# Strassen-like down products: seven block products for eight in four feed-forward groups

## The reference

```
h = rmsnorm(x, norm_ffn[i])
gu = h @ ffn_w_in[i]                       # 1024 -> 2 x 2816
x = x + (silu(gu[:, :2816]) * gu[:, 2816:]) @ ffn_w_out[i]
```

## Time and profile before

| | |
|---|---|
| median of 3 runs | 2080.69 us (2080.11 to 2082.2) |
| span of the profiled execution | 2080.3 us |
| PE busy | 2041.6 us, 98% |
| DVE busy | 965.7 us, 46% |
| ACT busy | 780.6 us, 38% |
| POOL busy | 324.6 us, 16% |
| mean granted TensorE clock | 0.997 |

### The profile page before, as it was taken

How to read it: one execution, slowest core, us unless ns; L and a number is a source line. 1 busy time by engine, 2 the same in 40 slices (tenths; PEclk the granted TensorE clock), 3 DMA queues, 4 the chain that set the end, 5 groups by cost and what they waited for, 6 DMA issues and landing times.

```text
span 2080.3 us, 26716 instructions
## 1 busy us (share of the span) xinstructions
PE 2041.6 (98%) x10149; PEld 1656.0 (80%) x10149; DVE 965.7 (46%) x1969; ACT 780.6 (38%) x1552; POOL 324.6 (16%) x497
## 2 busy tenths in 40 slices
PE   7999999999999999999999999999998999999998
PEld 6887888888888886788888888888787888777766
DVE  5437434443354345435534443364435664535455
ACT  4226332222232222333322222243337884435453
POOL 1103100000011120000110000041003764312211
PEclk9999999999999999999999999999999999999999
DMA  5330243333324331133243333225321103423212
GB/s 179 104 99 11 63 133 95 99 91 101 93 81 142 91 101 41 53 99 97 69 132 99 97 96 99 93 83 160 119 75 58 32 22 102 114 74 109 66 47 81
DMA packets 96910, 187.32 MB, mean 90 GB/s; under 512 B 8423, under 2 KB 16655, under 8 KB 96656
## 3 DMA queue, kind: packets, MB, share of 16 engines
q1 hardware_dynamic: 90432, 164.35, 26.3%
q0 software_dynamic: 6352, 21.27, 3.2%
HBM read 181.33 MB, written 4.26 MB: 89 GB/s over the span
## 4 chain that ended last, share of the span: by engine, by line
PE 90%; ACT 5%; DVE 2%; issue 1%; POOL 1%; DMA 0%; SPq 0%; ACTq 0%; DVEq 0%; POOLq 0%
PE bank L754 62%; PE bank L790 9%; PE bank L1265 5%; PE bank L1024 2%; PE bank L1186 1%; PE bank L1163 1%; PE bank L828 1%; PE bank L1279 1%; ACT sc L1808 1%; PE bank L1009 1%; PE bank L1095 1%; PE bank L1302 1%; PE bank L853 1%; ACT xn L1802 1%; PE bank L1152 1%
## 5 line engine op out<-in xcount | busy, mean ns | idle before, releaser
L1979 DVE TENSOR_TENSOR wl<-raw,wh 128x1024 fp32r<-128x1024 f32 x306 | 376.7, 1235 | 771.9 <-ACT wh L1382 770.9
L1382 ACT ACTIVATE wh<-raw 128x1024 fp32r<-128x1024 f32 x306 | 320.9, 1053 | 827.3 <-PE bank L754 785.5
L754 PE MATMUL bank<-hTh,wh 128*128 128x512 f32 (+2 forms) x1200 | 467.5, 390 | 0.2 <-issue 0.2
L754 PE MATMUL bank<-hTl,wh 128*128 128x512 f32 (+2 forms) x1200 | 466.9, 389 | 0.0
L754 PE MATMUL bank<-hTh,wl 128*128 128x512 f32 (+2 forms) x1200 | 466.9, 389 | 0.0
L754 PEld LDWEIGHTS bank<-hTh,wh 128*128 128x128 f32 (+2 forms) x1200 | 223.9, 187 | 48.7 <-issue 0.3
L754 PEld LDWEIGHTS bank<-hTh,wl 128*128 128x128 f32 (+2 forms) x1200 | 223.9, 187 | 48.2
L754 PEld LDWEIGHTS bank<-hTl,wh 128*128 128x128 f32 (+2 forms) x1200 | 223.9, 187 | 47.9
L754 PE MATMUL bank<-wh,hTh 128*128 128x512 f32 x400 | 156.5, 391 | 0.1
L754 PE MATMUL bank<-wh,hTl 128*128 128x512 f32 x400 | 155.7, 389 | 0.0
L754 PE MATMUL bank<-wl,hTh 128*128 128x512 f32 x400 | 155.6, 389 | 0.0
(11 more groups left out here) (383 smaller groups left out, 3105.5 us busy)
## 6 DMA issues: line engine op xcount, KB each, us to landing
raw<-in_ffn_w_in SPq DMA_DIRECT2D x88, 512.0 KB, 3.7
raw<-in_ret_w_in SPq DMA_DIRECT2D x48, 512.0 KB, 3.8
raw<-in_ffn_w_out SPq DMA_DIRECT2D x44, 512.0 KB, 3.7
raw<-in_diff_w_in SPq DMA_DIRECT2D x32, 512.0 KB, 3.7
raw<-in_fox_w_in SPq DMA_DIRECT2D x24, 512.0 KB, 4.1
raw<-in_nsa_w_in SPq DMA_DIRECT2D x20, 512.0 KB, 3.7
raw<-in_ret_w_out SPq DMA_DIRECT2D x16, 512.0 KB, 3.7
raw<-in_fox_w_out SPq DMA_DIRECT2D x8, 512.0 KB, 3.7
```

The source lines that it names most:

```text
L754: i = pe.do.matmul(dst, x, y, start=first and k == 0 and q == 0, stop=stop)
L1382: act.do.activation(M.hl[n % HL_SLOTS][0][:, 0:m], M.raw[n % RAW_SLOTS][:, 0:m], ACT.Copy).then_inc(*T.up("act_hi", n))
L1979: dve.do.tensor_tensor(wl[:, 0:m], M.raw[n % RAW_SLOTS][:, 0:m], wh[:, 0:m].bitcast(F32), ALU.subtract).then_inc(*T.up("dve_lo", n))
```

## The change

For groups 1 to 4 of each layer the product A (512 tokens x 512 hidden) by B (512 x 1024) is cut into 2 x 2 blocks each way, A in blocks of 256 x 256 and B in blocks of 256 x 512, and the four blocks of the result are made of seven block products, in Winograd's form:

- DVE makes sums of weight blocks: T1 = B12 - B11, T2 = B22 - T1, T3 = B22 - B12, T4 = B21 - T2, in place in the raw buffers, T2 in a buffer `form`. Four loads make seven chunks to split, in the order B11, T2, T1, B21, T3, B22, T4. A raw buffer is held until the last chunk that it carries is split.
- DVE makes sums of blocks of `f.pr`, S1 to S4, in place; ACT and DVE split each as before. For the first two tiles of a take only the first 256 tokens need `ah` and `al` then.
- PE works seven steps of 12 matmuls (2 token tiles x 2 x 3) into three pairs of banks: X for steps 0 and 3, Y for 1, 4 and 6, W for 2 and 5. A bank goes on being summed into from step to step, and DVE reads it after each step: step 0 goes to a buffer `alpha`, the others to `X`. `alpha` is summed over the four groups and added to `X` by six additions ahead of down(5).
- In DVE's program the four sums follow up(g)'s last split, the low halves of S1 and S3 stand ahead of step 0's evictions of down(g - 1), those of S2 and S4 ahead of step 1's, and a split follows each step's two evictions.

The core of the diff:

```diff
+SEVENS = (1, 2, 3, 4)
+STEPS = (("X", "A11"), ("Y", "S2"), ("W", "S1"), ("X", "A12"), ("Y", "S3"), ("W", "S4"), ("Y", "A22"))
+INTO = ("alpha", (0, 1), (2, 1), (0, 0), (2, 1), (0, 1), (2, 0))
+SUMS = {"T1": ("B11", "B12", "B11", "B11"), "T2": ("form", "B22", "B11", "T1"), "T3": ("B12", "B22", "B12", "B12"),
+        "T4": ("B21", "B21", "form", "T2")}
+QUADS = ("B11", "B12", "B22", "B21")
+SEVEN = ("B11", "T2", "T1", "B21", "T3", "B22", "T4")
+HELD = {"B11": "T1", "B12": "T3", "B22": "B22", "B21": "T4"}
+AFTER = {"B11": ("T1", "T2", "T3"), "B21": ("T4",)}
...
+    def seven(name, r0, rows, halves):
+        first, n = len(loads), len(chunks)
+        where = {q: first + k for k, q in enumerate(QUADS)}
+        last = {q: n + SEVEN.index(HELD[q]) for q in QUADS}
+        for q in QUADS:
+            loads.append((name, r0 + rows * (int(q[1]) - 1), rows // 128, (halves[int(q[2]) - 1],), last[q]))
+        for form in SEVEN:
+            chunks.append((rows // 128, halves[0][1], where, form, n))
...
@@ ffn(): down(g) of weight_chunks
+            if g in SEVENS:
+                seven(f"ffo{i}", c0, 256, ((0, 512), (512, 512)))
+                return
...
@@ ffn buffers
+        f.s = {form: [(sb(stack, "sh", [128, 2, 256], F32R), sb(stack, "sl", [128, 2, 256], F32R)) for _ in range(2)]
+               for form in ("S1", "S2", "S4")}
+        f.alpha, f.form = sb(stack, "alpha", [128, 2, S]), sb(stack, "form", [128, 1024])
...
@@ load_weights(n)
-            sp.wait_ge(*at("act_hi", n - RAW_SLOTS))
-            sp.wait_ge(*at("dve_lo", n - RAW_SLOTS))
+            last = LOADS[n - RAW_SLOTS][4]
+            sp.wait_ge(*at("act_hi", last))
+            sp.wait_ge(*at("dve_lo", last))
+            if CHUNKS[last][3] is not None:
+                sp.wait_ge(*at("dve_form", (CHUNKS[last][4], "T3")))
...
+def pe_seven(pe, T, M, tag, operand, ready):
+    first4, next4 = pe.banks4(), pe.banks4()
+    banks = T.bank[tag] = {"X": first4[0:2], "Y": first4[2:4], "W": next4[0:2]}
+    seen = {}
+    for j, (where, form) in enumerate(STEPS):
+        n = pe.use
+        pe.use += 1
+        wh, wl, nk = chunk_views(M, n)
+        h, l = operand(form)
+        for r in range(2):
+            b, cols = banks[where][r], slice(r * 128, r * 128 + 128)
+            if where in seen:
+                pe.wait_ge(*T.at("dve_seven", (tag, seen[where], r)))
+            else:
+                pe_bank(pe, T, b)
+            pe_weights(pe, T, n)
+            for name, key in ready(form):
+                pe.wait_ge(*T.at(name, key))
+            for k in range(nk):
+                for q, (x, y) in enumerate([(h[:, k, cols], wh[:, k, :]), (h[:, k, cols], wl[:, k, :]), (l[:, k, cols], wh[:, k, :])]):
+                    end = k == nk - 1 and q == 2
+                    i = pe.do.matmul(M.bank[b][:, :], x, y, start=where not in seen and k == 0 and q == 0, stop=end, skip_group_check=True)
+            i.then_inc(*T.up("pe_product", (tag, j, r), *[("chunk", n)] * r))
+            pe.free[b] = [("dve_seven", (tag, j, r))]
+        seen[where] = j
...
+def seven_form(f, g, form):
+    a, b = f.ah[g % 2], f.al[g % 2]
+    if form in f.s:
+        return [x[:, :, :] for x in f.s[form][g % 2]]
+    ks, ts = {"A11": (0, 0), "A12": (2, 0), "S3": (0, 256), "A22": (2, 256)}[form]
+    return a[:, ks:ks + 2, ts:ts + 256], b[:, ks:ks + 2, ts:ts + 256]
...
@@ act_ffn, take_up and the stage of g
-            act.do.activation(f.ah[g % 2][:, o, :], f.pr[:, o, :], ACT.Copy).then_inc(*up("act_ah", (i, g, o)))
+                act.wait_ge(*at("pe_product", down_end(i, g - 2)))
+            n = S // 2 if g in SEVENS and o < 2 else S
+            act.do.activation(f.ah[g % 2][:, o, 0:n], f.pr[:, o, 0:n], ACT.Copy).then_inc(*up("act_ah", (i, g, o)))
+    def high(g, form):
+        act.wait_ge(*at("dve_sum", (i, g, form)))
+        act.do.activation(seven_form(f, g, form)[0], seven_sum(f, form), ACT.Copy).then_inc(*up("act_s", (i, g, form)))
-        for half in range(2):
-            act_product(act, T, M, FFG[g - 1][1] // 256)
+        splits = 7 if g - 1 in SEVENS else FFG[g - 1][1] // 128
+        for c in range(splits):
+            if g in SEVENS and c < 2:
+                for form in (("S1", "S3"), ("S2", "S4"))[c]:
+                    high(g, form)
+            act_split(act, T, M)
...
@@ dve_split
+    for form in AFTER.get(CHUNKS[n][3], ()):
+        dve_sum(dve, T, M, n, form)
+def dve_sum(dve, T, M, n, form):
+    nk, width, where, own, first = CHUNKS[n]
+    x, y = SUMS[form][1:3]
+    for q in (x, y):
+        if q in where:
+            dve.wait_ge(*T.at(f"raw{where[q] % RAW_SLOTS}", where[q]))
+    dve.wait_ge(*T.at("dve_lo", n))
+    if form != "T1":
+        dve.wait_ge(*T.at("dve_form", (first, {"T2": "T1", "T3": "T2", "T4": "T2"}[form])))
+    if form == "T2" and dve.formed is not None:
+        dve.wait_ge(*T.at("dve_lo", dve.formed + SEVEN.index("T2")))
+        dve.wait_ge(*T.at("dve_form", (dve.formed, "T4")))
+    out, a, b = (form_buffer(M, where, q)[:, 0:nk * width] for q in (SUMS[form][0], x, y))
+    dve.do.tensor_tensor(out, a, b, ALU.subtract).then_inc(*T.up("dve_form", (first, form)))
+    if form == "T4":
+        dve.formed = first
...
@@ dve_ffn
+            if g - 1 in SEVENS:
+                dve.wait_ge(*at("dve_s", (i, g - 1, "S4")))
-            dve.do.tensor_tensor(f.al[g % 2][:, o, :], f.pr[:, o, :], f.ah[g % 2][:, o, :].bitcast(F32), ALU.subtract).then_inc(
+            n = S // 2 if g in SEVENS and o < 2 else S
+            dve.do.tensor_tensor(f.al[g % 2][:, o, 0:n], f.pr[:, o, 0:n], f.ah[g % 2][:, o, 0:n].bitcast(F32), ALU.subtract).then_inc(
                 *up("dve_al", (i, g, o)))
+    def sums(g):
+        q11, q12, q21, q22 = (f.pr[:, k:k + 2, t:t + 256] for t in (0, 256) for k in (0, 2))
+        dve.wait_ge(*at("dve_al", (i, g, 3)))
+        dve.do.tensor_tensor(q22, q21, q22, ALU.add).then_inc(*up("dve_sum", (i, g, "S1")))
+        dve.wait_ge(*at("dve_sum", (i, g, "S1")))
+        dve.do.tensor_tensor(q21, q11, q21, ALU.subtract).then_inc(*up("dve_sum", (i, g, "S3")))
+        dve.wait_ge(*at("dve_sum", (i, g, "S3")))
+        dve.do.tensor_tensor(q11, q22, q11, ALU.subtract).then_inc(*up("dve_sum", (i, g, "S2")))
+        dve.wait_ge(*at("dve_sum", (i, g, "S2")))
+        dve.do.tensor_tensor(q12, q12, q11, ALU.subtract).then_inc(*up("dve_sum", (i, g, "S4")))
+
+    def low(g, form):
+        h, l = seven_form(f, g, form)
+        dve.wait_ge(*at("act_s", (i, g, form)))
+        dve.do.tensor_tensor(l, seven_sum(f, form), h.bitcast(F32), ALU.subtract).then_inc(*up("dve_s", (i, g, form)))
+
+    def evict(g, j, r):
+        tag = f"down{i}{g}"
+        where = STEPS[j][0]
+        src = M.bank[T.bank[tag][where][r]][:, :]
+        dve.wait_ge(*at("pe_product", (tag, j, r)))
+        if INTO[j] == "alpha":
+            if g == SEVENS[0]:
+                dve.do.tensor_copy(f.alpha[:, r, :], src).then_inc(*up("dve_seven", (tag, j, r)))
+            else:
+                dve.wait_ge(*at("dve_seven", (f"down{i}{g - 1}", j, r)))
+                dve.do.tensor_tensor(f.alpha[:, r, :], f.alpha[:, r, :], src, ALU.add).then_inc(*up("dve_seven", (tag, j, r)))
+            return
+        t, half = INTO[j][0] + r, INTO[j][1]
+        xs = M.X[:, t, half * 512:half * 512 + 512]
+        dve_x_newest(dve, T, t)
+        dve.do.tensor_tensor(xs, xs, src, ALU.add).then_inc(*up("dve_seven", (tag, j, r)))
+        dve.x[t] = ("seven", (tag, j, r))
+
+    def merge(t):
+        r, tag = t % 2, f"down{i}{SEVENS[-1]}"
+        dve.wait_ge(*at("dve_seven", (tag, 0, r)))
+        for half in ((1,), (0, 1))[t // 2]:
+            xs = M.X[:, t, half * 512:half * 512 + 512]
+            dve_x_newest(dve, T, t)
+            dve.do.tensor_tensor(xs, xs, f.alpha[:, r, :], ALU.add).then_inc(*up("dve_x", (f"merge{i}", t, half)))
+            dve.x[t] = (f"merge{i}", t, half)
 
...
@@ dve_ffn, the loop over g
     for g in range(1, 6):
         dve_product(dve, T, M, 4)
         dve_product(dve, T, M, 4, 4, take_up(g))
+        if g in SEVENS:
+            sums(g)
+        if g - 1 in SEVENS:
+            for j in range(7):
+                if g in SEVENS and j < 2:
+                    for form in (("S1", "S3"), ("S2", "S4"))[j]:
+                        low(g, form)
+                for r in range(2):
+                    evict(g - 1, j, r)
+                dve_split(dve, T, M)
+            continue
         for half in range(2):
             dve_product(dve, T, M, FFG[g - 1][1] // 256, 4, dve_add(dve, T, M, f"down{i}{g - 1} {half}", half))
+            if g in SEVENS:
+                for form in (("S1", "S3"), ("S2", "S4"))[half]:
+                    low(g, form)
+    for t in range(4):
+        merge(t)
     if i == 0:
         a, b = (dve_add_and_scale(dve, T, M, "n2", f"down05 {half}", half) for half in range(2))
```

More of the change, by code:

```diff
@@ L70, with plain @@
 FFG = [(0, 256)] + [(256 + g * 512, 512) for g in range(5)]
-def weight_chunks():
-    chunks = []
```

(53 more changed lines are left out.)

22 lines of the change are left out of this document (14 added, 8 removed).

## The result

| | before | after |
|---|---|---|
| median, four runs each | 2081.28 us | 2101.59 us |
| ratio to before, 95% interval | | 1.0093 [1.0081, 1.0105] |
| span of the profiled execution | 2080.3 | 2101.6 |
| PE busy | 2041.6 | 2035.0 |
| DVE busy | 965.7 | 1097.2 |

A forecast was written before the change was run, and what follows sets the result against it. PE bounds the feed-forward, but in changed down stages DVE's queue of evictions holds it. Terms 17.4 - 2.5 + 1.9 = +16.8 us on 2080.3 gave 2097.1, stated as 2097.5; range 2084 to 2107, with rivals 2080 to 2110.

The forecast's parts named there:

- DVE's queue: Full down stage: takes, sums, low halves, evictions and splits timed from the up product's end; step 4's eviction at 21.05 us.
- Waits ahead of steps 3, 4 and 6, none ahead of 5: Full down stage: PE waits for DVE's evictions to free banks, about 3 us ahead of step 3, again before 4 and 6.
- +2.98 a full stage, +2.5 the first: Changed down stages that also hold sums and low halves: PE leaves 2.98 us later, in layer 0's first 2.5.
- -1.23 a fourth stage: Each layer's last changed stage, in group 5, without sums or low halves: PE leaves 1.23 us sooner, -2.5 for two.
- T1 to T3 at nothing: Gate product's last slot: three weight sums, 3.7 us, fit where DVE idles 4.2 us, so they cost nothing.
- Layer 0's tail +1.9: Last down of layer 0: alpha merges delay the first tile's additions and norm, stalling PE's transpose by 1.9 us.
- Layer 1's tail: nothing: Last down of layer 1: the merges' delay costs nothing, as a wait for PE's second tile lies before the norm.
- The price of chaining: DVE's queue: a 128x512 op waiting for the one before costs 0.72 to 0.73 us against 0.60; without it 2094.5 us.
- Rival (c): Clock falls after PE's wait before step 3: +1 to +3 us in six stages, 2104 to 2116 us; chance 0.11.
- If the granted clock falls: Full down stage: one of the listed signs that the forecast is wrong, TensorE's granted clock falling.
- (a): Full stages: evictions come in time, PE never waits, -22.0 + 1.9, so 2060.6 us, faster; chance 0.13.
- (b): Full stages: DVE's queue 2.5 to 3 us shorter through cheaper sums and takes, about the same, 2081 us; chance 0.08.

The follow-up runs named there:

- t4_early: Changed kernel with activation sums behind the seven steps, alpha merges split around tile 0's additions, and T4 formed one slot sooner on DVE: 2060.71 us, 0.9895 of before.
- own_bank: Changed kernel with a pair of banks of its own for step 6, no longer waiting for step 4's eviction: 2096.06 us, 1.0071 of before.
- late_sums: Changed kernel with only the four activation sums and their eight halves moved behind the seven steps: 2069.61 us, 0.9941 of before.
- no_t123: Changed kernel without T1, T2 and T3, T4 staying as B21 - B12: 2100.58 us, 1.0091 of before.
- no_t4: Changed kernel without T4, B21 split and used in its place: 2090.38 us, 1.0044 of before.
- spread: Changed kernel with the six alpha merges moved from ahead of the last down's additions to just ahead of each token tile's: 2103.19 us, 1.0104 of before.
- pool_t4: Changed kernel with activation sums behind the seven steps, alpha merges split around tile 0's additions, and T4 on POOL: 2067.62 us, 0.9932 of before.
- only_four: Changed kernel with seven products in group 4 alone, groups 1 to 3 by eight products: 2086.03 us, 1.0019 of before.

## Why the prediction was right, and where its sizes were off

- **A matmul saved is 0.229 us, 2.75 a stage.** Right: t4_early shows exactly that once nothing waits, 62.75 for 65.50.
- **DVE's queue.** Right, op by op: the takes began at -1.88 (said: -1.94), the sums at 6.61 (6.54), step 0's eviction at 10.60 (10.53), step 4's at 21.13 (21.05). The sums cost like low halves, 0.68 to 0.69, chained 0.73.
- **Waits ahead of steps 3, 4 and 6, none ahead of 5.** Right where the clock stays up: 3.19, 0.51, 1.22 us. In the four stages where it fell PE waits ahead of steps 3 and 6 alone, and leaves at the same time. own_bank shows that step 6 waits for the bank of step 4, late_sums that the order of DVE's queue sets how long.
- **+2.98 a full stage, +2.5 the first, -1.23 a fourth stage.** Measured 3.00 to 3.02, 2.39, -1.22 and -0.94; in layer 1's fourth stage PE waited 0.44 us ahead of step 3, which I had not in the sum.
- **T1 to T3 at nothing.** Right (no_t123), and T4 at its full length (no_t4: 1.3 us a group, said 1.27).
- **Layer 0's tail +1.9.** It was +2.15; the stall itself was 1.88.
- **Layer 1's tail: nothing.** Wrong, +1.87 us; the step that failed is "a wait for PE's second tile lies between, so nothing". I compared the first tile's norm with DVE's additions and left out who stands between them. The root there is a chain of ten small ops on POOL, two norms deep. Its first op for tile 0 began at 1399.17, which is 9.7 us after the start of the last down (7.4 before the change), and DVE's scaling waited for its last one until 1404.96; PE waited 0.31 us. From then on POOL is the one that is late. PE's four transposes began 16.5, 25.6, 31.9 and 38.3 us after the start of the last down before the change, and 17.0, 26.3, 33.3 and 40.1 after. With the merges spread over the tiles (spread) the chain began at 7.4 again and 1.27 of the 1.87 us were back. The chain of waits in the changed kernel runs over POOL in this stretch:

```profile
1411.81 2.46 POOL cells L516
...
1414.34 0.58 POOL cells L518
...
1415.02 2.16 POOL cells L520
```

In the kernel before the ops of L516 and L520 (L460 and L464 there) took 0.30 and 0.34 us in the median. But in this very stretch its ops were long too, up to 2.28 us: all forty took 22.4 us there and 24.8 after. That DVE's crowded queue makes POOL's small ops long is suggested by pool_t4, not shown here.

- **The terms and the rest.** 2.39 + 3.02 + 3.01 + 3.01 + 3.00 + 3.02 = 17.45 (said 17.4); -2.16 (-2.5); 2.15 (1.9); 1.87 (0). That is 19.3 of the 21.3 us. The other 2.0 are the two stretches without changed work; of the 4.5 us by which the spans differ more than my sum of 16.8, they and layer 1's tail make 3.9. In the sparse attention's start the clock was at 0.50 from 1600 to 1610, as it had been 0.67 after the long wait before; how long it stays low there differs between executions, and what of the 1.26 us it makes up is not settled.
- **The price of chaining.** The trace sides with the earlier trace rows: 452.20 to 452.92 is 0.72 for an op of 0.68 that the next waits for, against 0.60 from 454.99 to 455.59, between two ops of the same size in SBUF that do not wait. The Trainium skill (VectorE: DVE Perf Modes, section The DRAIN you can't avoid) has it that a semaphore behind each op costs nothing extra. The trace does not agree where the next op waits for it: 0.12 us each here.
- **Rival (c), and a sign of being wrong that came.** "If the granted clock falls" stands among the signs of being wrong, and it fell in four of the six full stages: in four of the five in which PE had idled 3.2 us, and not in the first, after 2.59. So half of rival (c) came true, and the forecast's time held because the price in these stages was nought, for the reason that own_bank shows. I had reckoned with six slow microseconds and an extra of 1 us or more; a spell was some eight matmuls long, and the waits ahead of steps 4 and 6 took in what it cost. The Trainium skill (TensorE: Matmul & The Clock Gate, section HAM oscillation) puts a limit to the idle gaps of PE, and the waits here stay under it. So the prediction's step from that page to "(c) would hold in every full stage" was not sound. Nor does the trace agree with the limit: the clock fell behind four of these shorter waits.
- **Rivals (a) and (b)** fell with the queue as worked out. The time of (a), 2060.6, is what t4_early reached with 2060.71, once the evictions do start in time; that the two agree to a tenth is luck, since its tails differ from (a)'s terms.

## What to carry to other kernels

Fewer products on the busiest engine are worth what the queue that must empty their banks allows: list that queue op by op from the last moment at which it was idle, and look at when it reaches the eviction that PE waits for, not at the engine's share. Before giving up such a change, move everything in that queue that nobody waits for yet behind the evictions, and into idle slots; here the same work in another order turned +1% into -1%. A stretch that hangs on a chain of small ops on a third engine has no slack but that engine's own.

## What the runs showed of the hardware that I had not expected

- TensorE's granted clock fell to 1.2 GHz behind some stalls of PE and not behind others of the same length. After 3.2 us it fell in 18 of 20 places (4 of 5 in the changed kernel and in own_bank, 5 of 5 in no_t123 and in spread), after 2.6 us in one of four, after 1.9 us in 3 of 9 (two stages of no_t4 and late_sums' tail; not in the tails of the changed kernel, no_t4 and no_t123), after 2.10 us in only_four's tail, and after 1.2 to 1.4 us never. After 1.24 us in the kernel before it did not either. PE had been fully busy ahead of each of these stalls.
- One POOL op of 128x1024 f32 in SBUF (2.40 us) lengthened a DVE op with two SBUF inputs from 0.42 to 1.67 us, and left the one that reads PSUM at 0.68.
